# Dilated attention's two coarse groups in parity order: half of their score columns computed, transposed and multiplied

## What is computed

```python
DILATED_GROUPS = ((128, 1), (512, 4), (2048, 16))      # (window, dilation); half = window // (2 * dilation) = 64
a = pa.reshape(B, S, 3, N_GROUPS_A, HEADS_PER_GROUP_A, HEAD_DIM_A)
for g, (window, dil) in enumerate(DILATED_GROUPS):
    o, lse = dilated_group_attention(a[:, :, 0, g], a[:, :, 1, g], a[:, :, 2, g],
                                     bias_groups[:, g], dil, window // (2 * dil))
...
wgt = jax.nn.softmax(jnp.stack(lses, axis=0), axis=0)
o_a = jnp.sum(wgt[..., None] * jnp.stack(outs, axis=0).astype(jnp.float32), axis=0)
```

## Time and profile before

| | before |
|---|---|
| median of 3 runs | 2096.0 us (2094.89 to 2096.01) |
| the profiled execution's own time | 2093.91 us |
| its span, first to last instruction | 2092.1 us |
| TensorE matmuls (PE) busy | 2026.6 us, 97% of the span |
| VectorE (DVE), ScalarE (ACT) busy | 1328.5 us (64%), 919.9 us (44%) |
| mean granted TensorE clock | 0.994 |
| score(0) to the end of head 7 | 1604.74 to 1762.79 us of the span |

### The profile page before, as it was taken

The page is one execution under the profiler, slowest core; times in us unless marked ns, Lnnn a source line. Parts: engine busy times, 40 slices in busy tenths (PEclk is TensorE's granted clock), DMA queues, the critical chain, the costliest instruction groups (busy, mean ns, idle before and its releaser), DMA issues.

```text
span 2092.1 us, 28840 instructions
## 1 busy us (share of the span) xinstructions
PE 2026.6 (97%) x12264; PEld 1775.3 (85%) x12264; DVE 1328.5 (64%) x1306; ACT 919.9 (44%) x863; POOL 45.9 (2%) x43
## 2 busy tenths in 40 slices
PE   8999999998999999999999999999989999999998
PEld 7988888897888888888978788789979878998997
DVE  6665766798666877567665856644444556665444
ACT  5344433375433644434344333343434446554343
POOL 0000000000000000000000000100010000001000
PEclk9999999999999999999999999999999999999999
DMA  8444555445554535454534545335556453344442
GB/s 327 162 161 161 186 196 201 167 162 201 182 186 169 187 121 197 185 201 181 201 122 170 206 178 201 141 131 185 191 193 199 146 153 121 121 161 151 181 180 101
DMA packets 32373, 364.34 MB, mean 174 GB/s; under 512 B 3677, under 2 KB 3938, under 8 KB 10130
## 3 DMA queue, kind: packets, MB, share of 16 engines
q1 hardware_dynamic: 28146, 347.49, 45.3%
q0 software_dynamic: 4128, 15.39, 3.0%
HBM read 361.77 MB, written 1.10 MB: 173 GB/s over the span
## 4 chain that ended last, share of the span: by engine, by line
PE 83%; DVE 9%; ACT 5%; DMA 2%; issue 1%; SPq 0%; DVEq 0%; ACTq 0%
PE acc L920 27%; PE bank L832 9%; PE bank L834 9%; PE bank L833 9%; PE bank L1502 9%; PE bank L1504 4%; PE bank L871 2%; PE bank L873 2%; PE bank L872 2%; ACT w_hi L1806 2%; DMA raw<-slabs_in 1%; DVE w_lo L2369 1%; DVE w_lo L2374 1%; PE bank L1642 1%; PE bank L1678 1%
## 5 line engine op out<-in xcount | busy, mean ns | idle before, releaser
L832 PE MATMUL bank<-ht_both,w_hi 128*128 128x256 f32 x1536 | 432.2, 281 | 2.7 <-DVE w_lo L2369 2.7
L834 PE MATMUL bank<-ht_both,w_lo 128*128 128x256 f32 x1536 | 429.7, 280 | 0.0
L833 PE MATMUL bank<-ht_both,w_hi 128*128 128x256 f32 x1536 | 429.1, 279 | 0.0
L2374 DVE TENSOR_TENSOR w_lo<-raw,w_hi 128x4096 fp32r<-128x4096 f32 (+4 forms) x83 | 310.2, 3737 | 119.5 <-ACT w_hi L1806 119.5
L1794 ACT ACTIVATE w_hi<-raw 128x2048 fp32r<-128x2048 f32 x166 | 309.4, 1910 | 146.2 <-PE bank L834 142.7
L1806 ACT ACTIVATE w_hi<-raw 128x4096 fp32r<-128x4096 f32 (+4 forms) x91 | 283.5, 3115 | 181.8 <-PE bank L1504 156.7
L832 PEld LDWEIGHTS bank<-ht_both,w_hi 128*128 128x128 f32 x1536 | 288.9, 188 | 7.0 <-DVE w_lo L2369 3.3
L833 PEld LDWEIGHTS bank<-ht_both,w_hi 128*128 128x128 f32 x1536 | 289.0, 188 | 1.5 <-issue 0.5
L834 PEld LDWEIGHTS bank<-ht_both,w_lo 128*128 128x128 f32 x1536 | 289.2, 188 | 0.0
L2369 DVE TENSOR_TENSOR w_lo<-raw,w_hi 128x2048 fp32r<-128x2048 f32 x98 | 220.0, 2288 | 94.6 <-ACT w_hi L1794 94.5
L1502 PE MATMUL bank<-ht_both,w_hi 128*128 128x512 f32 x768 | 269.1, 393 | 0.0
(11 more groups left out here) (411 smaller groups left out, 3196.4 us busy)
## 6 DMA issues: line engine op xcount, KB each, us to landing
raw<-slabs_in SPq DMA_DIRECT2D x147, 2048.0 KB, 7.7
raw<-slabs_in SPq DMA_DIRECT2D x23, 1024.0 KB, 6.7
raw<-slabs_in SPq DMA_DIRECT2D x12, 512.0 KB, 11.3
g_tab<-gains_in POOLq DMA_DIRECT2D x11, 512.0 KB, 4.4
a_bias<-bias_rows POOLq DMA_DIRECT2D x8, 576.0 KB, 7.6
b_tab<-gains_in POOLq DMA_DIRECT2D x8, 512.0 KB, 5.1
raw<-slabs_in SPq DMA_DIRECT2D x2, 1152.0 KB, 5.9
raw<-slabs_in SPq DMA_DIRECT2D x1, 1280.0 KB, 5.9
```

The source lines that it names most:

```text
L832: nc.tensor.matmul(o, whi, xhi, start=first, stop=False)
L833: nc.tensor.matmul(o, whi, xlo, start=False, stop=False)
L834: return nc.tensor.matmul(o, wlo, xhi, start=False, stop=last)
L2374: nc.vector.tensor_tensor(w_lo[ring][:, 0:w], raw[ring][:, 0:w], w_hi[slot][:, 0:w].bitcast(F32), ALU.subtract).then_inc(lo_ready, 1)
```

## The change

Groups 1 and 2 ("coarse") are held with the tokens in parity order: the 128 even ones first, then the 128 odd ones (the queries, of all groups, in that order and then reversed). Group 0's keys and values stay in the order of time.

- ScalarE writes queries and coarse keys in parity order (`rows_a`), and writes the output `oa_hi` back in the order of time; VectorE likewise for `oa_lo`.
- The coarse values come out in parity order because the stationary operand of their projection takes every second token (`by_parity`). Slabs 0 and 2, which hold group 0 and group 1, therefore take two matmuls of 256 columns, one with 128 neighbouring tokens and one with every second, where one of 512 stood.
- Of the coarse scores only the blocks of equal parity are computed: four matmuls of 128 columns, both groups in one bank. A head's scores are 512 columns wide for each half of the queries, not 768, and so are the addition, maximum, exponential, scaling and the transposes (8, not 12). The coarse products with the values are four matmuls of 128 columns.
- Each head takes two banks less of the rotation. The bias of a head comes by two transfers (257 elements of stride 1 from every second row offset, and two blocks of 128).

```diff
+                            if i == 1:
+                                m = nc.tensor.matmul(psum(*key)[:, :], by_parity(x[:, k, :], t), w[:, a:a + 512],
+                                                     start=first, stop=last)
+                            else:
+                                nc.tensor.matmul(psum(*key)[:, 0:S], x[:, k, c], w[:, a:a + S], start=first, stop=False)
+                                m = nc.tensor.matmul(psum(*key)[:, S:2 * S], by_parity(x[:, k, :], t),
+                                                     w[:, a + S:a + 2 * S], start=False, stop=last)
...
-                    for g in range(A_G):
-                        key = ("as", hd, g)
-                        wait_free(*key)
-                        c = 2 * g + hd % 4 // 2
-                        for t in range(TT):
-                            m = nc.tensor.matmul(psum(*key)[:, t * S:(t + 1) * S],
-                                                 a_qk[hd // 4][r, c, t * P:(t + 1) * P],
-                                                 a_qk[hd // 4][r, 2 * A_G + c, :], start=True, stop=True)
-                        m.then_inc(bank_full[ticket[key][0]], 1)
...
+                    for t in range(TT):
+                        for g in (1, 2):
+                            o = t * S + (g - 1) * P
+                            m = nc.tensor.matmul(psum(*key)[:, o:o + P], q[r, 2 * g + c, t * P:(t + 1) * P],
+                                                 q[r, 2 * A_G + 2 * g + c, (1 - t) * P:(2 - t) * P],
+                                                 start=True, stop=True)
...
-                    for g in range(A_G):
-                        pe.wait_ge(*read("at", hd, g))
-                        for kb in range(2):
-                            m = nc.tensor.matmul(psum(*key)[r:r + 64, 0:S], a_v[:, kb, g, hd * 64:(hd + 1) * 64],
-                                                 a_pt[:, g, kb * S:(kb + 1) * S],
-                                                 start=g == 0 and kb == 0, stop=g == A_G - 1 and kb == 1)
...
+                    pe.wait_ge(*read("at", hd, 1))
+                    for g in (1, 2):
+                        for t in range(TT):
+                            o = (g - 1) * S + t * P
+                            m = nc.tensor.matmul(psum(*key)[r:r + 64, t * P:(t + 1) * P],
+                                                 a_v[:, 1 - t, g, hd * 64:(hd + 1) * 64],
+                                                 a_pt[:, 1, o:o + P],
+                                                 start=False, stop=g == 2 and t == 1)
...
+                    rows, source = a_qk[half][:, 2 * u:2 * u + 2, :], pair(psum(*key))
+                    if u != A_G:
+                        rows = rows.rearrange("p c (r a) -> p c a r", r=2)
+                        source = source.rearrange("p c (a r) -> p c a r", r=2)
```

More of the change, by code:

```diff
@@ L283, in program @@
         ar = ExitStack()
-        a_p = [sb(f"a_p{i}", [P, TT, A_G, S], F32, ar) for i in range(2)]
+        a_p = [sb(f"a_p{i}", [P, TT, 2 * S], F32, ar) for i in range(2)]
         a_qk.append(sb("a_qk1", [P, 4 * A_G, S], F32, ar))
         a_v = sb("a_v", [P, TT, A_G, 512], F32, ar)
-        a_pt = sb("a_pt", [P, A_G, 512], F32, ar)
-        a_bias = [sb(f"a_bias{i}", [P, A_G, 384], F32, ar) for i in range(2)]
+        a_pt = sb("a_pt", [P, 2, 512], F32, ar)
+        a_bias = [sb(f"a_bias{i}", [P, S + 8 + 2 * P], F32, ar) for i in range(2)]
         a_nm = sb("a_nm", [P, 2, 2], F32, ar)
@@ L535, in program @@
             take("aq", 0, u)
-        for g in range(A_G):
+        for g in range(2):
             take("as", 0, g)
@@ L1607, in rows_a, with by_parity @@
                     up_pair(("aq", half, u), g, (c, c + P), KD, 512, ht_hi, ht_lo)
+                def by_parity(columns, t):
+                    return columns.rearrange("p (a r) -> p r a", r=2)[:, t, :]
                 def values_a(i, t):
-                    need(g0 + AV_SLAB[i])
-                    tokens(("av", i, t), g0 + AV_SLAB[i], t, 512, KD, 512, 0, ht_hi, ht_lo)
+                    g, key, c = g0 + AV_SLAB[i], ("av", i, t), slice(t * P, (t + 1) * P)
+                    need(g)
+                    wait_free(*key)
+                    for k in range(KD):
+                        need_ht(k)
+                        for x, w in ((ht_hi, w_hi[g % 2]), (ht_hi, w_lo[g % RING]), (ht_lo, w_hi[g % 2])):
+                            a = k * 512
+                            first, last = k == 0 and x is ht_hi and w is w_hi[g % 2], k == KD - 1 and x is ht_lo
+                            if i == 1:
[5 more added lines that the diff above has]
+                                                     w[:, a + S:a + 2 * S], start=False, stop=last)
+                    m.then_inc(bank_full[ticket[key][0]], 1)
                 def rows_b(s, t):
@@ L2215, in exps @@
                     for t in range(TT):
-                        rows = a_p[hd % 2][:, t, :, :]
+                        rows = a_p[hd % 2][:, t, :]
                         ins = nc.scalar.activation(rows, rows, ACT.Exp, bias=a_nm[:, hd % 2, t:t + 1],
@@ L2238, in hybrid @@
                     act.wait_ge(*full(*key))
[L2239 removed]
+                    by_query = oa_hi[r:r + 64, hd // 2, :].rearrange("p (a r) -> p r a", r=2)[:, ::-1, ::-1]
+                    nc.scalar.activation(by_query, psum(*key)[r:r + 64, 0:S].rearrange("p (r a) -> p r a", r=2), ACT.Copy)\
                         .then_inc(oa_hi_ready, 1)
@@ L2924, in biased @@
                     if hd >= 2:
[L2925 to L2934, removed]
+                        dve.wait_ge(*full("at", hd - 2, 1))
+                    dve.wait_ge(bias_loaded[hd % 2], 32 * (hd // 2 + 1))
+                    key = ("as", hd, 0)
+                    row = a_bias[hd % 2][:, 0:S]
+                    window = bass.AP(row.tensor, row.offset, [row.ap[0], (1, TT), (1, S)])
+                    dve.wait_ge(*full(*key))
+                    nc.vector.tensor_tensor(p[:, :, 0:S], pair(psum(*key)), window, ALU.add).then_inc(read_sem(*key), 1)
+                    key = ("as", hd, 1)
+                    blocks = a_bias[hd % 2][:, S + 8:2 * S + 8].unsqueeze(1).to_broadcast([P, TT, S])
+                    dve.wait_ge(*full(*key))
+                    nc.vector.tensor_tensor(p[:, :, S:2 * S], pair(psum(*key)), blocks, ALU.add)\
+                        .then_inc(read_sem(*key), 1)
+                    for g in range(2):
                         dve.wait_ge(*read("as", hd, g))
-                    nc.vector.tensor_reduce(a_nm[:, hd % 2, :], p[:, :, :, :].rearrange("p t g s -> p t (g s)"), AX_X,
-                                            ALU.max, negate=True).then_inc(a_max, 1)
+                    nc.vector.tensor_reduce(a_nm[:, hd % 2, :], p[:, :, :], AX_X, ALU.max, negate=True)\
+                        .then_inc(a_max, 1)
                 def normed(hd):
@@ L3145, in constants @@
         valid = (rel % dilation == 0) & (np.abs(rel) <= 64 * dilation)
-        for m in range(2 * S - 1):
-            c[bucket[m] if valid[m] else N_BUCKETS, C_HOT + 512 * g + m] = 1.0 if valid[m] else NEG
+        for i, m in enumerate(range(2 * S - 1) if g == 0 else range(1, 2 * S - 1, 2)):
+            c[bucket[m] if valid[m] else N_BUCKETS, C_HOT + 512 * g + i] = 1.0 if valid[m] else NEG
     return c
```

53 lines of the change are left out of this document (35 added, 18 removed).

## The result

The changed kernel took 2081.19 us (median of 4 runs, 2079.46 to 2082.38) beside 2095.44 for the kernel before, ratio 0.9937 with a 95% interval of 0.9925 to 0.995. A second comparison, of five rounds, gave 2081.28 against 2094.53, ratio 0.9934 (0.9921 to 0.9948). So the change makes the kernel faster by 0.63 to 0.66%, 13.3 to 14.3 us. The prediction was 2079.2, in a range of 2076.5 to 2086.5. The median is 2.0 us above the forecast, inside the range and 0.2 outside the forecast's own narrow range (2077.5 to 2081).

The account below looks back on a forecast made before the run. TensorE, busy 97% of the span, was taken to bound the kernel. Savings of 14.2 + 3.1 - 0.24 - 0.3 = 16.8 us gave 2077.1 profiled and a median of 2079.2 us, range 2076.5 to 2086.5.

Parts of the forecast that it names:

- The thinnest cover: Behind head 7, branch B's transposes wait for VectorE's rope; 0.9 us of slack before, about 0.5 predicted to stay.
- The fourth rival: TensorE shortens its own cover, above all ahead of the rope; 1 us wait per head, 8 us: 2087; 5 in 100.
- Scores and products: Branch A's eight heads: narrower coarse records save 0.90 us of scores and 0.88 of products a head, 14.2 us.
- the prediction's bounds: Limits on the saving from half-width score and product records over eight heads: 13.4 and 14.8 us.
- Transposes: Four fewer records a head save 0.44 us, nothing at head 7, where the product waits for ScalarE's first copy: 3.1 us.
- Value projections: Slabs 0 and 2: four projections with 48 matmuls of 256 columns instead of 24 of 512 cost 0.24 us more.
- I take nothing: Stride-two stationary loads of the value projections were priced at no cost; bound 11.3 us more if a load doubled.
- rival 2: Strided loads in the value projections cost double, leaving a gain of 5.5 us, 2090.5; 6 in 100.
- the other ground: SBUF rule: a 16-byte line hit twice gives full bandwidth, so value-projection loads at stride two float32 lose nothing.
- Rival 3: Slow strided loads in value projections of slabs 0 to 2 make the change lose, from 272 ns a load; 5 in 100.
- The copies: ScalarE's last query/key copy before the first scores: interleaved writes cost 0.3 us, between nothing and 0.6 if doubled.
- Rival 1: Score and product records don't halve, lasting as long as a load's record, 187 and 137 ns: 2084.7; 8 in 100.

Follow-up runs that it names:

- The doubled scores: Changed kernel with each head's twelve score records issued twice in a row into the same banks; a head's batch took 3.71 us, the stretch grew by 17.3 us.
- the versions without the waits: Changed kernel with first scores behind a value projection and a later wait for values: 2078.19 us, ratio 0.9922; with ScalarE's copies in two planes too: 2077.29, 0.9915.

## Why the prediction was right, and what was off

**The bound.** TensorE and nothing else: right. Nobody else became late. The thinnest cover, ahead of branch B's transposes, was given 0.5 us; VectorE's rope was ready at 1776.49 and TensorE came at 1776.9, 0.4 us. The probabilities of head 4 were scaled by 1702.04 and asked for at 1704.79, 2.75 us for a forecast of 2.6. The fourth rival did not come, except as waits that were there before: the two for ScalarE's copies, one of which grew, and the one at head 7.

**Scores and products, 14.2 us forecast, 13.45 measured** (products 8 x 2.73 less 15.08, scores 22.37 less 15.68, heads 0 and 1 being 0.04 longer each). That half the width takes about half the time was right; the size was off by 0.8 us. The forecast took the middle between "everything halves" and "the 17 and 13 ns more here are a fixed cost of each record", 120 and 117 ns in place of 232 and 228, so 112 and 111 saved for each of 128 records. The doubled scores show 216 ns for a whole record and 111 for a half one, 105 saved, and the excess over 216 paid once for a batch. Since a head has 12 records of scores and 12 of products before and after, the excess stays whole wherever it sits; the half of it that the middle gave away was the error. The measured value also lies under the prediction's bounds when they are worked out from its own prices: 125 and 120 ns give 8 x 1.72 = 13.8, and 116 and 114 give 14.7, where it has 13.4 and 14.8. That its 13.4 is so near to 13.45 is a slip of the sum and not a forecast; the last 0.3 us are the half records, 111 ns and not half of 215.

**Transposes, 3.1 forecast:** 7 x 0.44 and 0.09 at head 7, 3.2. The reason given for head 7 (the product waits for the first copy) is what its chain shows.

**Value projections, 0.24 more forecast, 0.6 measured** (0.32 on slabs 0 and 1, 0.15 and 0.16 on slab 2's two), for split and stride together; the stride's part is between 0.4 and 1.24, by the pace that the plain loads would have had. "I take nothing" for the stride was nearly right, but a free stride on VectorE was no ground for it: at four elements TensorE's loads cost nearly what rival 2 said for two, 113 ns for each of 96, and the change would have gained 4.4 us of its stretch (158.05 to 153.7). What held was the other ground, two hits to a line. Rival 3 needed a load of 272 ns, 2.3 of the steps of 118. Load records of 298 to 317 ns were seen, but records of 188 already fit in steps of 118, and what counts is the step: it reached 0.24 us, 2.0 of them, so even there the change would not have lost.

**The copies, 0.3 forecast, 0.46 measured:** interleaved writes take 1.06 for 0.60, nearly the double that was the upper end.

**Rival 1 fell:** half records do last half, 111 for 216 ns, with a load in each. The Trainium skill's rule that a load overlaps running matmuls only in other row groups (TensorE: Matmul & The Clock Gate, on packing small matmuls) does not describe these rows (the same section elsewhere also allows a load into a background weight buffer, which no run here singles out): the records of 188 ns stood in steps of 111 to 120.

**The sum.** The parts of the prediction leave 141.0 us for the stretch (158.05 - 14.2 - 3.1 + 0.24; the copy lies ahead of it), and not the 141.5 that it names; measured were 142.47, 1.5 more. Net from the norm's transposes to the gates 15.05 us (197.10 to 182.05), forecast 16.8: 0.75 from the records, 0.4 from projections, 0.2 from the copy, and 0.4 from two projections beside heads 0 and 2 that took 5.45 us in the kernel before and 5.66 now, the two paces of the plain loads again, for which no run gives a cause. The rest between 15.05 and the 13.3 to 14.3 of the medians is not separated run by run. Two falls of the clock, seen in one of two profiles of the changed kernel and in neither of those of the versions without the waits, are of the right size; the mean clocks of the unprofiled executions go the same way, but where in them it fell isn't seen, so that these falls are the cause is argued, not shown.

## What to carry to other kernels

Price a batch of small matmuls as a fixed part for entering it plus a part by width, from two batches of different length; an average over one batch puts the fixed part where a cut seems to save it. When tokens are to be permuted nearly for nothing by reading the stationary operand at a stride, keep to two float32 elements and put the strided load behind a wide matmul. And look at the short waits of an engine that is busy 97% of the time: moving two of 1.3 and 0.9 us under a projection brought 2.3 us in the profiles and another 3 us in the median here (2081.28 to 2078.19, intervals that overlap); what goes beyond their own length may be the clock, which fell behind such waits in some executions.

## What the runs showed of the hardware that was not expected

- A stationary load of 128x128 fp32r takes 188, 198, 252, 309, 317 and 298 ns at strides of 1, 2, 3, 4, 8 and 16 elements; behind 256 columns what is above 198 stands in the steps (0.12, 0.18, 0.24, 0.24 and 0.22 us from a stride of two on), behind 512 nearly nothing of it does (48 matmuls in 11.21 us at two, 11.55 at four).
- ScalarE copies 128x512 float32 from PSUM to SBUF in 0.60 us when it reads at a stride of two, and in 1.06 us when it writes to two places 512 bytes apart in turn.
- Matmuls of 256 columns behind plain loads have two paces at a granted clock of 1.00: 118 ns a step in most projections, 113 in the values without a stride, in two projections beside heads 0 and 2 of the kernel before (5.45 us for 5.66), and in the first beside head 0 at strides of three and sixteen (5.65 for 5.85). The cause is open.
- The granted clock fell for a few us behind waits of TensorE as short as 0.9 us, though it had been busy for tens of us before: behind score(1) in three of the eleven profiled executions of the changed kernel and of its variants that keep both waits (to 0.50 over 4.81 us in the one shown), behind score(0) in one of them. In the one profile of the kernel before and in the two of the versions without the waits the clock stayed at 1.00 around these places.
